# Two more query and key pairs turned by VectorE, rounded running sums and later weight splits in a two-block transformer kernel

## The reference, cut to what matters

```python
def first_block(x, ...):
    h = rms_norm(x, mix_norm_g)
    ys, gate_logit = _token_mixers(h, w_in, ...)  # four kinds of attention
    branch = einsum('bsnc,ncd->bsnd', ys, w_branch)
    x = x + sum(sigmoid(gate_logit) * branch, axis=2) @ w_out
    h = rms_norm(x, mlp_norm_g)
    x = x + square(relu(h @ w_up)) @ w_down
    return rms_norm(x, final_norm_g)
def _stick_breaking(q_blk, k, v, dist):
    z = einsum('bqhd,bshd->bhqs', q_blk, k) * (HEAD_DIM ** -0.5)
    log_keep = where(strict, log_sigmoid(-z), 0.0)
    log_between = cumsum(log_keep, axis=3, reverse=True) - log_keep
    a = where(strict, exp(log_sigmoid(z) + log_between), 0.0)
    return einsum('bhqs,bshd->bqhd', a, v)
def second_block(x, ...):
    proj = rms_norm(x, norm1_g) @ w_in      # q, k, v and the input of a convolution
    x = x + concat([moba_attention(q, k, v), conformer_conv(u)]) @ w_out
    h = rms_norm(x, norm2_g)
    return x + (silu(h @ w_gate) * (h @ w_up)) @ w_down
```

## Time and profile before

| | |
|---|---|
| median of 3 runs | 773.12 us (773.03 to 773.34) |
| the profiled execution: its time, its span | 773.35 us, 771.5 us |
| TensorE busy (matmuls) | 760.8 us, 99% |
| VectorE, ScalarE, GpSimd busy | 582.8 us, 408.6 us, 49.3 us |
| granted TensorE clock | 1.000 |

### The profile page before, as it was taken

One profiled execution on the slowest core, in us unless ns is written; L12 is line 12 of the kernel. 1 busy time (PEld: TensorE's weight loads), 2 busy tenths in 40 slices (PEclk: granted clock), 3 DMA queues, 4 the chain that ended last, 5 costly groups with the idle time before them and its releaser, 6 DMA issues.

```text
span 771.5 us, 9633 instructions
## 1 busy us (share of the span) xinstructions
PE 760.8 (99%) x3712; PEld 636.2 (82%) x3712; DVE 582.8 (76%) x945; ACT 408.6 (53%) x555; POOL 49.3 (6%) x42
## 2 busy tenths in 40 slices
PE   8989999999999999999999999999999999999998
PEld 6878899888888888888888887888988888888886
DVE  5698688697757878687778838699857777768584
ACT  7666255456657546545454546764665344353430
POOL 0200000000001500000000005041000000000000
PEclk9999999999999999999999999999999999999999
DMA  9953434454544467665665567655133665655601
GB/s 334 391 175 110 136 110 142 159 168 161 163 164 164 159 204 249 192 216 175 208 205 179 173 207 273 218 172 164 56 110 109 222 215 181 200 184 199 206 13 54
DMA packets 68508, 137.28 MB, mean 178 GB/s; under 512 B 2544, under 2 KB 6256, under 8 KB 67824
## 3 DMA queue, kind: packets, MB, share of 16 engines
q1 hardware_dynamic: 68032, 135.30, 52.6%
q10 hardware_dynamic: 432, 1.38, 0.5%
HBM read 135.48 MB, written 1.05 MB: 177 GB/s over the span
## 4 chain that ended last, share of the span: by engine, by line
PE 85%; DVE 8%; DMA 3%; ACT 2%; SPq 1%; issue 1%; ACTq 0%
PE b L652 19%; PE b L654 18%; PE b L653 18%; PE SS L652 4%; PE SS L654 4%; PE SS L653 4%; DVE wlo L1605 2%; PE TT L621 2%; PE OO L652 2%; PE OO L654 2%; PE OO L653 2%; DMA cs<-in_cst 2%; DVE ca L2128 2%; DMA xr<-in_x 1%; PE b L814 1%; PE SS L761 1%
## 5 line engine op out<-in xcount | busy, mean ns | idle before, releaser
L1605 DVE TENSOR_TENSOR wlo<-raw,whi 128x2048 fp32r<-128x2048 f32 (+2 forms) x119 | 269.9, 2270 | 80.3 <-ACT whi L1144 79.5
L1144 ACT CAST whi<-raw 128x2048 fp32r<-128x2048 f32 (+2 forms) x119 | 222.9, 1878 | 124.4 <-PE b L654 81.9
L652 PE MATMUL b<-whi,Ahi 128*128 128x512 f32 (+2 forms) x520 | 206.7, 398 | 2.9 <-ACT gates L1217 2.4
L654 PE MATMUL b<-whi,Alo 128*128 128x512 f32 (+2 forms) x520 | 199.8, 384 | 0.0
L653 PE MATMUL b<-wlo,Ahi 128*128 128x512 f32 (+2 forms) x520 | 199.1, 383 | 0.0
L652 PEld LDWEIGHTS b<-whi,Ahi 128*128 128x128 f32 x520 | 97.8, 188 | 21.1 <-ACT gates L1217 2.9
L654 PEld LDWEIGHTS b<-whi,Alo 128*128 128x128 f32 x520 | 97.6, 188 | 19.9
L653 PEld LDWEIGHTS b<-wlo,Ahi 128*128 128x128 f32 x520 | 97.9, 188 | 17.8
L1993 DVE STREAM_TRANSPOSE hT<-ust 32x256 f32<-32x256 f32 (+1 forms) x192 | 81.5, 425 | 2.8
L652 PE MATMUL b<-whi,Bhi 128*128 128x512 f32 x154 | 60.5, 393 | 0.1
L654 PE MATMUL b<-whi,Blo 128*128 128x512 f32 x154 | 60.0, 390 | 0.0
(11 more groups left out here) (295 smaller groups left out, 1095.1 us busy)
## 6 DMA issues: line engine op xcount, KB each, us to landing
raw<-in_w_in SPq DMA_DIRECT2D x38, 1024.0 KB, 5.1
raw<-in_w_up SPq DMA_DIRECT2D x16, 1024.0 KB, 5.4
raw<-in_w_dn SPq DMA_DIRECT2D x16, 1024.0 KB, 5.1
raw<-in_w_d SPq DMA_DIRECT2D x11, 1024.0 KB, 5.0
raw<-in_w_g SPq DMA_DIRECT2D x10, 1024.0 KB, 5.0
raw<-in_w_u SPq DMA_DIRECT2D x10, 1024.0 KB, 5.1
raw<-in_w_out SPq DMA_DIRECT2D x8, 1024.0 KB, 5.1
raw<-in_w_br SPq DMA_DIRECT2D x4, 1024.0 KB, 5.0
```

The lines of the kernel that those rows point to most:

```text
L652: e.matmul(dst, xh, H[:, kc, c0:ce], start=first and kc == krs[0], stop=False)
L654: ins = e.matmul(dst, xl, H[:, kc, c0:ce], start=False, stop=last and kc == krs[-1])
L1144: e.copy(whi[:, s, 0:m], raw[:, r, 0:m]).then_inc(s_hi, 1)
L1605: e.tensor_tensor(wlo[:, s, 0:m], raw[:, r, 0:m], whi[:, s, 0:m].bitcast(F32), ALU.subtract).then_inc(s_lo, 1)
```

## The change

First projection: pairs 0 and 2 (queries and keys of the stick-breaking heads) join `VP`. The heads start in slots 11, 13, 17, 19 instead of 8, 9, 14, 15. The running sum's fp32 matmul of 384 columns becomes two fp32r matmuls on a rounded high part (`sh`, ScalarE) and a rest (`sd`, VectorE). The tables that heads need are loaded ahead of unit 7 with a semaphore of their own. At the start the first piece comes in two halves and VectorE rounds it. Second block: the final gain is multiplied on GpSimd after the roots; the square of the final norm becomes a weighted sum on VectorE with the squared gain, made by ScalarE in the MLP; splits of units 86 to 95 stand later in the streams; some taps move; `ln_back` stands in the middle of a product; the residual's scaling joins its addition.

```diff
-VP = {4: (9, 10, 11, 12), 6: (13, 14, 15, 16), ...
+VP = {0: (6, 6, 7, 8), 2: (8, 9, 9, 10), 4: (9, 10, 11, 12), 6: (13, 14, 15, 16), ...
-    for h, a in enumerate((8, 9, 14, 15)):
-        for k, name in ((0, "sz"), (1, "sm"), (2, "ss"), (4, "sc"), (5, "su"), (6, "sp"), (7, "so")):
+    for h, a in enumerate((11, 13, 17, 19)):
+        for k, name in ((0, "sz"), (1, "sm"), (2, "ss"), (3, "sh"), (4, "sc"), (5, "su"), (6, "sp"), (7, "so")):
-    for s, n in ((10, 8), (12, 2), (14, 4), (16, 3), (18, 3)):
+    for s, n in ((10, 8), (12, 2), (14, 3), (16, 3), (18, 2)):
         bg[s].append(("cv", n))
...
+        first = min(groups[t] for t in unit_of if unit_of[t] == i)
+        if i >= unit_of["p2", 4, 1, 0]:
+            ahead = {unit_of["p2", 4, 1, 0]: 6, unit_of["wo2", 0, 0, 0]: 5, unit_of["wo2", 0, 1, 0]: 3}
+            g = max(g, first - ahead.get(i, 4))
+            if i > unit_of["wo2", 1, 1, 0]:
+                g = max(free_at[i - NSPL], first - 4 - max(0, i - unit_of["u", 0, 0, 0]) // 2)
         g = max([g] + [h + 1 for h in split_after])
...
+        e.dma_start(raw[:, 0, 0:256], units[0][0][:, 0, 0:256]).then_inc(d_piece[0], 16)
         load_xt(0)
...
+            if i == NRAW + 3:
+                o = CST["MB"][0]
+                e.dma_start(cs1[:, o:N1], cst_d[:, N0 + o:N0 + N1]).then_inc(d_cs0, 16)
...
         def sc(h, s):
-            e.matmul(R[:, 0:384], c1("LG"), L, start=True, stop=False)
+            Lh, Ll = sum_split(h)
+            w.wait_ge(s_sh, h + 1)
+            e.matmul(R[:, 0:384], LGr[:], Lh, start=True, stop=False)
+            w.wait_ge(s_sd, h + 1)
+            e.matmul(R[:, 0:384], LGr[:], Ll, start=False, stop=False)
...
+        def sh(h):
+            if h == 0:
+                e.copy(LGr[:], c1("LG")).then_inc(s_lg, 1)
+            e.copy(sum_split(h)[0], Sb[:, h % 2, 384:768]).then_inc(s_sh, 1)
...
+        def sd(h):
+            Lh, Ll = sum_split(h)
+            w.wait_ge(s_sh, h + 1)
+            e.tensor_tensor(Ll, Sb[:, h % 2, 384:768], Lh.bitcast(F32), ALU.subtract).then_inc(s_sd, 1)
...
-                if (n, t) == (1, 0):
-                    ln_back(0)
-                    ln_back(1)
+                product(("wo2", 0, n, t), ..., between=ln_backs if (n, t) == (1, 0) else None)
...
-                    for t_, n_ in ORD:
-                        fin_square(t_, n_)
...
+        w.wait_ge(d_piece[0], 32)
+        e.tensor_copy(whi[:, 0, 0:512], raw[:, 0, 0:512]).then_inc(s_hi, 1)
...
+        def square_sum(t, n):
+            w.wait_ge(s_g2, 1)
+            w.wait_ge(s_sq, SQ["N2", t, n] + 1)
+            return own(e.tensor_tensor_reduce(sq, sq, g2row[:, 512 * n:512 * n + 512], 1.0, 0.0, ALU.mult, ALU.add, ...))
...
-        before("wo2", 0, 0, 0)
         for k in range(10):
...
-            conv(6 if k < 4 else 4 if k < 8 else 1)
+            conv(6 if k < 5 else 4 if k < 8 else 1)
+        before("wo2", 0, 0, 0)
...
+        root("r3", r3_, smx["r3"][1], 2)
+        root("r4", smx["r4"][2], smx["r4"][1], 2)
         for t, n in ORD:
             xs = xr[:, t, 512 * n:512 * n + 512]
-            w.wait_ge(s_sq, SQ["N2", t, n] + 1)
-            w.wait_ge(s_xt, XT["N2", t, n] + 1)
             e.tensor_tensor(xs, xs, par2[:, 512 * n:512 * n + 512], ALU.mult).then_inc(s_pg, 1)
-        root("r3", r3_, smx["r3"][1], 2)
-        root("r4", smx["r4"][2], smx["r4"][1], 2)
```

More of the change, by code:

```diff
@@ L207, in build @@
         gap = ExitStack()
+        with ExitStack() as r5:
+            LGr = sb("LGr", [128, 128], F32R, c=r5)
         gates = sb("gates", [128, 2, 4096], c=gap)
@@ L212, in build @@
         Sb = sb("Sb", [128, 2, 768], c=r1)
+        with ExitStack() as r5:
+            LH = sb("LH", [128, 2, 768], F32R, c=r5)
         PT = sb("PT", [128, 2, 768], c=r1)
@@ L393, in build @@
             g = free_at[i - NSPL]
+        first = min(groups[t] for t in unit_of if unit_of[t] == i)
[4 more added lines that the diff above has]
+                g = max(free_at[i - NSPL], first - 4 - max(0, i - unit_of["u", 0, 0, 0]) // 2)
         g = max([g] + [h + 1 for h in split_after])
+        assert g <= first - 3, (i, g, first)
         split_after[g] = i
@@ L422, in build, with sum_split @@
                                          + [("N2", t, n) for t, n in ORD]
-                                         + [("F", t, n) for t, n in ORD]
                                          + [("N3", t, n) for t, n in ORD])}
+    def sum_split(h):
+        return LH[:, h % 2, 0:384], LH[:, h % 2, 384:768]
     nsq = nlf[:].rearrange("p t x -> p (t x)")
@@ L497, in read_out @@
         mine = [i for i, q in enumerate(QP) if q[0] <= c]
-        return [(s_tp, max([TP[i] + 1 for i in mine if i in TP])),
+        return [(s_tp, max([0] + [TP[i] + 1 for i in mine if i in TP])),
                 (s_vt, max([0] + [list(VP).index(QP[i][2]) + 1 for i in mine if i not in TP]))]
@@ L630, in _, with product @@
         count = [0]
-        def product(tag, hi, lo, k0, t, bank_of, first, last, kr=None, at=None, cols=None):
+        def product(tag, hi, lo, k0, t, bank_of, first, last, kr=None, at=None, cols=None, between=None):
             assert groups[tag] == count[0], (tag, count[0])
@@ L644, in product @@
                 for kc in krs:
+                    if between and kc == 2:
+                        between()
                     if at and kc in at:
@@ L1083, in ln_back, with ln_backs @@
             gone[NBK[p]] = (s_ln, 2)
+        def ln_backs():
+            ln_back(0)
+            ln_back(1)
         for n in range(2):
@@ L1090, in _ @@
                 clear(bk)
-                product(("wo2", 0, n, t), Bhi, Blo, 0, t, lambda c0, bk=bk: bank[bk], True, False)
+                product(("wo2", 0, n, t), Bhi, Blo, 0, t, lambda c0, bk=bk: bank[bk], True, False,
+                        between=ln_backs if (n, t) == (1, 0) else None)
                 if (n, t) == (0, 0):
@@ L1181, in _ @@
             input_hi(k)
-            piece_hi(k // 4, k % 4)
+            if k:
+                w.wait_ge(s_hi, 1)
+                piece_hi(k // 4, k % 4)
         for k in range(4):
@@ L1394, in _ @@
                     hidden_hi(j - 1)
+                if j == 3 and q == 0:
+                    w.wait_ge(d_par2, 16)
+                    e.activation(g2row, par2[:, 0:1024], ACT.Square).then_inc(s_g2, 1)
                 if q == 3:
@@ L1405, in _ @@
                 relu2(j, 1)
-        def fin_square(t, n):
-            w.wait_ge(s_pg, ORD.index((t, n)) + 1)
-            square("F", t, n, xr[:, t, 512 * n:512 * n + 512], o4)
         def turn2(t, n):
@@ L1656, in _ @@
             piece_lo(3, k)
+            if k == 1:
+                w.wait_ge(s_rs, RS["r1"] + 1)
+                e.tensor_scalar(r1q, r1_, 0.125, None, ALU.mult)
+                e.tensor_scalar(r1d, r1_, 32 ** -0.5, None, ALU.mult).then_inc(s_r1s, 1)
         w.wait_ge(d_par, 16)
@@ L1925, in residual @@
             xs = xr[:, t, 512 * n:512 * n + 512]
+            if base == 8:
+                e.scalar_tensor_tensor(out=xs, in0=xs, scalar=r3_[:, t:t + 1], in1=bank[W_ACC[t, n]], op0=ALU.mult,
+                                       op1=ALU.add).then_inc(s_res, 1)
+                return
             e.tensor_tensor(xs, xs, bank[W_ACC[t, n]], ALU.add).then_inc(s_res, 1)
@@ L2049, in stats2 @@
             variance("r4", v, sm_, D)
-            for t in range(2):
-                ins = e.tensor_scalar(xr[:, t, :], xr[:, t, :], r3_[:, t:t + 1], None, ALU.mult)
-            k_x = own(ins)
+            before("p2", 0, 0, 1)
             w.wait_ge(s_rs, RS["r4"] + 1)
             e.tensor_tensor(r4_, r3_, r, ALU.mult).then_inc(s_rv, 1)
-            return k_x
         def r0(i):
```

41 lines of the change are left out of this document (29 added, 12 removed).

## The result

| | before | after |
|---|---|---|
| median | 773.11 us (773.03 to 773.34) | 781.51 us (780.73 to 783.18) |
| the profiled execution: time, span | 773.35, 771.5 | 781.43, 779.3 |

The ratio is 1.0109, interval 1.0096 to 1.0122: slower by 8.4 us, where 4.4 were forecast and 781.0 was the upper end of the range. The direction was right, the size was not.

What follows compares the result with a forecast made beforehand. TensorE, busy 99% of the span, bounds the kernel. New p1 losses of 9.0 us less 4.8 saved give +4.2; with -0.9, +1.8 and -0.7 that is +4.4, so 777.5 us against the median; range 771.0 to 781.0.

Steps and rivals of the forecast that it cites:

- The stream of VectorE hangs on the landing: p1: VectorE's stream, walked from split 4 at 25.56, follows unit 4's landing, not TensorE, so TensorE's earlier gains can't help.
- (1): p1: two pair turns leave TensorE, 0.45 us each, saving 0.9 us.
- (2): p1: the running sum's fp32 matmul becomes two fp32r ones, saving 0.30 us a head, 1.2 us for four heads.
- (3): p1, start of slot 12: the 2.7 us loss behind `evac`, caused by late tables, goes.
- rival B: ScalarE isn't late at slot 16, p1 losses are 5.4, split 86's move costs nothing: 771.8 us, the same; chance 0.15.
- A: Rival: VectorE keeps up, no stands in p1; faster, 766.4 us, or 768.5 with the split 86 delay; chance 0.13.
- (4): Second block: GpSimd's gain products move behind the roots, so VectorE's subtraction is no longer held: -0.9 us.
- (7): Second block, wo2: `ln_back` in mid-product starts ScalarE's chain 1.36 us sooner: -0.7 us.
- (5): Second block: split 86, moved behind product 175, holds the square of `r0(2)`; the turn of rotary part 2 comes 1.7 us later.
- (6): Second block: splits 87 and 88 leave the stretch ahead of `am(0)`, two taps precede `am(7)`; product at 555.02 late, +1.8 us.
- Rival C: p1 as forecast, but the square of `r0(2)` isn't held: 775.4 us; chance 0.19.
- Rival D: VectorE stays behind, TensorE waits again in slots 18 to 40, 3.5 us per further late `evac`: 781 us; chance 0.11.

Runs made afterwards that it cites:

- Experiment 8: Kernel before with only pairs 0 and 2 turned by VectorE and heads in slots 11, 13, 17, 19; 780.11 us, ratio 1.0093.
- experiment 1: Changed kernel with pairs 0 and 2 turned by TensorE again, all else kept; 774.62 us, ratio 1.0017.
- experiment 11: experiment 7 without its sixteen matmuls, with heads in slots 13, 15, 18, 20 and eight matmuls ahead of the first product; 777.37 us, ratio 1.0055.
- experiment 2: Changed kernel with GpSimd's memsets of the query and key tiles waiting for the two scaled roots; 781.47 us, ratio 1.0108.
- experiment 3: Changed kernel with sixteen unread matmuls filling TensorE's idle time before the scores of head 0; 782.52 us, ratio 1.0124.
- experiment 4: Changed kernel with split 86 back behind product 174 (6 slots ahead instead of 5); 778.56 us, ratio 1.0070.
- experiment 7: Changed kernel, pairs still on VectorE, with memsets after the roots, sixteen idle-time matmuls, and start and split 86 as before; 778.30 us, ratio 1.0072.
- experiment 9: experiment 5 with eight instead of six matmuls ahead of the first product; 771.37 us, ratio 0.9981.
- experiment 5: Changed kernel with three parts undone: pairs 0 and 2 on TensorE, split 86 and the first piece's load and rounding as before; 771.57 us, ratio 0.9982.
- experiment 6: experiment 5 with `evac(3, 0)` ahead of the rounding of unit 9 on ScalarE; 773.28 us, ratio 0.9993.
- experiment 10: experiment 9 with head 1 in slot 14 instead of 13; 773.79 us, ratio 1.0010.
- experiment 12: experiment 5 with the heads in slots 10, 12, 16, 18; 770.29 us, ratio 0.9958.

## Why the prediction was wrong, step by step

**Right: the bound, and the mechanism in p1.** TensorE stands for a VectorE that has been given more than it can do. Experiment 8 shows the pairs, with the heads that they ask for, as the cause by themselves, experiment 1 as the cause within the change, and experiment 11 that it is a backlog: moving the scores away doesn't cure it.

**The step that failed: "The stream of VectorE hangs on the landing".** I took split 4 as bound by ScalarE's rounding of unit 4 "on the landing" at 23.61, and VectorE's start at 25.56, and walked on from there. I didn't ask what the rounding is queued behind, and whether the change gives that a new wait. It does: `evac(0, 0)` now reads the scaled roots, and these were held by GpSimd's zeroing. Nor did I ask whether the landing stays where it was. It doesn't: with the changed start unit 4 lands at 24.00 to 24.70 (changed kernel, experiments 1 to 4), with the start of the kernel before at 23.30 to 23.73 (all others). In experiment 3, where the roots hold nothing, ScalarE's rounding stands for the landing as before, 0.4 later than 23.61:

```profile
24.03 1.91 ACT L1177 CAST whi<-raw 128x2048 fp32r<-128x2048 f32 x1 [1.13 <-DMA raw<-in_w_in]
```

That the walk was else right is seen by comparing two rows in every version of the changed kernel that has the pairs on VectorE and the heads where the change puts them: the start of split 4 on VectorE, and the start of ScalarE's `evac(3, 0)`, which frees slot 16.

| kernel | split 4 | evac(3, 0) | distance |
|---|---|---|---|
| forecast | 25.56 | 59.25 | 33.7 |
| 7, premises | 25.27 | 59.31 | 34.04 |
| 3, filled wait | 25.97 | 60.01 | 34.04 |
| 2, roots first | 26.20 | 60.25 | 34.05 |
| 4, split 86 | 26.67 | 60.70 | 34.03 |
| after | 27.67 | 61.71 | 34.04 |

Whether the clock fell before slot 12 (after, 2, 4) or not (3, 7), and whether slot 4 came on time or 2 us late, the distance is the same. The row of the changed kernel in ScalarE's timeline, with the four parts of the move in one:

```profile
61.71 1.56 ACT L1251 ACTIVATE gates<-b,st 128x256 f32<-128x256 f32 x4
```

(Experiment 8, which has the kernel before's running sums and so neither rounding nor rest of them in these streams, has 26.95 and 60.52, 33.6 apart.) So of the 3.2 us missing in p1, 2.1 are the anchor of the walk (27.67 against 25.56; 1.7 of it the roots, 0.4 the landing), 0.35 is the walk's length, and 0.7 the running sum in slot 21 that waits for a turned pair's move. ("Slots 18 to 24 find their splits and `evac`s within 0.3 us" looked at splits and accumulators, not at the banks of the sums.) The remaining 0.1 is `evac(3, 0)` itself: slot 16 starts 0.88 us behind its start, where 0.80 was forecast. All this is the profiled execution's account, and how much of the anchor is the roots changes from one to the next: the first one took 3.13 or 3.14 us in six of the nine kernels whose memsets don't wait for it, 1.12 in two, 0.23 in one, and in experiment 2 the median didn't gain by holding the memsets back. The Trainium skill (SBUF — State Buffer, SBUF: two separate sides) says that a GpSimd instruction holds the shared port pair for its whole length against a VectorE instruction in a two-port mode. I cited that section for the subtraction of 1.78 us and didn't apply it to the roots; 3.14 us beside the memsets and 0.16 without them (experiment 2) agree with it. Whether VectorE runs these two in such a mode no view shows, and they were held past the end of more than one memset (20.26 to 24.12).

**(1) Turns, right.** Between slots 4 and 28 sixteen transposes took 1.50 us from start to start, the eight that are left take 0.79; with 0.09 for each first matmul behind, 0.9 less. **(2) Running sums, too large:** an fp32r matmul of 384 columns is 0.17 us behind another, as forecast (61.35 to 61.52), but the first of each pair costs 0.24 on the mean. Four heads cost 2.57 us before and 1.64 after, summed from start to start: 0.9 instead of 1.2. **(3) The wait of 2.7 us** went. In experiment 9, with the change's order of loads, the tables of the heads land at 30.6 instead of 35.8, and the first mask isn't due before 42; by these times either of the two edits would have done.

**Losses in p1, by size.** Scores of head 0: 4.1 forecast, 4.3 measured. Slot 16: 3.5 forecast; 3.1 visible in experiments 3 and 7 (3.35 with the restart), 0.5 in the changed kernel, where the fall of the clock stood in its place. So rival B is refuted with A. The forecast has both at full clock and doesn't see the fall; that costs nothing at slot 12, and 0.8 behind slot 16 in experiment 7 (1.6, less the wait at slot 21).

**The start, given nothing ("0.3 us either way, covered by the wait for split 4"): too small, by the landing.** That slot 4 came 0.5 later is covered by the later waits, as forecast; that unit 4 lands 0.4 later isn't, since VectorE's stream hangs on it. Experiments 5 to 12 have the start of the kernel before or nearly, and slot 4 came between 0.1 early and 2.3 late. In a kernel with a stand further on (the tables before, the scores after) this is taken up; in experiments 5 and 9 nothing takes it up, and their executions spread by 2.9 and 2.4 us, where the kernel before spreads by 1.2 to 1.7. That the spread is the start's is argued from this, not shown.

**(4), (7) right:** -1.0 for -0.9, -0.9 for -0.7. **(5) and (6) right in the profile:** +1.8 for +1.8, by the square held in ScalarE's stream and a wait of 2.7 us before the turn; experiment 4 undoes just that. Rival C is refuted. What no term had is the clock behind this wait, 1.6 us more in those executions in which it fell; the profiled one of the changed kernel isn't among them. **"Everything else: 0"** was out by 0.3, two steps of 0.17 between slots 188 and 196, whose cause I haven't tested, and 0.3 more lie around the span (2.13 us after, 1.85 before).

The sum, then: +4.4 forecast, 2.1 for the anchor, 0.4 for the walk and the length of `evac`, 0.7 for slot 21, 0.1 for the second block as a whole (+0.3 where +0.2 was forecast), 0.3 around the span: 8.0 of the 8.1 between the two profiled executions. Rival D (further waits in slots 18 to 40) had the right size by a mechanism of which only the 0.7 of slot 21 took place.

A reading that was wrong without harm: other engines' streams are late "only at these places". The same view of waits has two more in the kernel before, 1.3 us for GpSimd's `Blo` ahead of the first matmul and 1.1 us before the first product.

What stays open: why slot 4 comes late in some executions. What differs there is TensorE's clock. The trace's first record of the clock, at full, lies between 4.2 and 4.9 us in the seven profiled executions whose slot 4 came at 16.50 to 17.10 (before, after, 3, 5, 9, 10, 11), and between 8.9 and 10.7 in the seven where it came at 17.97 to 18.89 (1, 2, 4, 6, 7, 8, 12); in the latter matmuls are 0.43 apart up to that record and 0.23 behind it. Why the clock rises late in some isn't known: filling 0.6 of the 1.2 us ahead of the first product changed nothing, and a stand of 0.66 was followed by fast matmuls (9), one of 0.89 by slow ones (12), one of 1.23 by fast ones (5).

## What to carry to other kernels

When a walk along an engine's queue starts at "the data landed", look at what stands in that queue ahead of the first instruction, whether the change gives it a new input, and whether the landing itself stays: a multiplication by a scale of two numbers moved a whole stream by 1.7 us, one more load at the start by 0.4. Compare absolute times at the places where two engines meet, not only the list of waits: a slow clock and a wait had changed places there, and filling the one brought back the other. Work given to an engine that is 76% busy on the mean is not free where it is full locally; shifting the one consumer that stands only shows the backlog at the next.

## What the hardware showed that I had not expected

- VectorE's instruction on 128 x 2 numbers took 3.14 us beside GpSimd's memsets, 1.12 or 0.23 in other kernels with the same code (experiments 4 and 6; 3), and 0.16 when the memsets waited (2, 7, 11). It ended with a memset each time that it was held, at 22.80 in experiment 4 (the second one's end, 22.77) and at 24.15 in the changed kernel (the fourth one's, 24.12).
- The granted clock fell to 0.50 behind stands of TensorE of 4.3 us each time (changed kernel, experiments 2, 4, 8), behind one of 3.1 in experiments 7 and 11 but not in experiment 3, behind one of 2.65 in experiments 1 and 3 but not in experiment 2, nor behind 2.67 in the changed kernel; it fell behind one of 1.90 in experiment 10, and not behind 3.0 in experiment 11 or 2.43 in the kernel before. So the length of the stand alone doesn't tell. The Trainium skill (TensorE: Matmul & The Clock Gate, Part 1: The HAM clock gate) says that the number of slow matmuls of one kernel changes from run to run; the start agrees. In experiment 12 (TensorE's timeline) the first product's matmuls are 0.43 apart up to 8.7 us:

```profile
5.13 1.19 PE L692 MATMUL SS<-whi,Ahi 128*128 128x512 f32 x2 [0.89 <-ACT whi L1181]
6.12 1.05 PE L695 MATMUL SS<-whi,Alo 128*128 128x512 f32 x2
6.97 1.05 PE L698 MATMUL SS<-wlo,Ahi 128*128 128x512 f32 x2
```

The view of windows prints a clock of 1.00 for such a start all the same (experiments 1, 2 and 12, windows of 1 us), because the trace has no record of the clock there; only the distances show it, and the time of the first record (9.1 us here).
